# VectorE alone forms the token block sums, a down tile precedes the last block product, eight banks for the last chunk pair

## The reference, cut to what matters

```python
xn = rms_norm(x, g_pre_mix)
z  = xn @ w_in                       # 1024 tokens, 1024 -> 8192 columns
y_attn = diff_attention(q, k, v)     # 8 heads, two score maps each, per-head norm
y_conv = gb * short_conv(gc * hc)
y_pool = multiscale_pool(u)
gates  = sigmoid(z[..., OFF_GATE:] + b_gate)
merged = gates0 * (y_attn @ w_attn_proj) + gates1 * (y_conv @ w_conv_proj) + gates2 * (y_pool @ w_pool_proj)
x  = x + rms_norm(merged @ w_out, g_post_mix)
hn = rms_norm(x, g_pre_ffn)
gu = hn @ w_gate_up                  # 1024 -> 2 * 2816
ff = (silu(gu[..., :D_FF]) * gu[..., D_FF:]) @ w_down
x  = x + rms_norm(ff, g_post_ffn)
```

## Time and profile before

| what | us |
|---|---|
| median of three runs | 1870.77 (1868.34 to 1870.95) |
| the profiled execution, whole | 1869.41 |
| its span, first to last instruction | 1867.8 |
| PE busy | 1799.5 (96%) |
| VectorE busy | 1148.4 (61%) |
| ScalarE busy | 688.1 (37%) |
| GpSimd busy | 258.8 (14%) |

### The profile page before, as it was taken

The page is one execution under the profiler, slowest core; times in us unless marked ns, Lnnn a source line. Parts: engine busy times, 40 slices in busy tenths (PEclk is TensorE's granted clock), DMA queues, the critical chain, the costliest instruction groups (busy, mean ns, idle before and its releaser), DMA issues. The chain is left out here.

```text
span 1867.8 us, 25127 instructions
## 1 busy us (share of the span) xinstructions
PE 1799.5 (96%) x8628; PEld 1485.1 (80%) x8628; DVE 1148.4 (61%) x1778; ACT 688.1 (37%) x1351; POOL 258.8 (14%) x502
## 2 busy tenths in 40 slices
PE   6999999999989999999999999899999999999987
PEld 5877777777867888888888888688888888788876
DVE  4218888888765774441646645955545454567666
ACT  4216666666633323342221133433333333212111
POOL 2211111111150001112100112500000000000002
PEclk9999999999999999999999999999999999999999
DMA  6221111111132213337535513122222221333332
GB/s 218 91 57 35 58 58 56 57 56 45 57 124 79 90 62 107 113 102 281 187 120 183 204 68 113 56 74 82 81 68 95 79 95 68 124 124 112 124 113 90
DMA packets 123088, 187.11 MB, mean 100 GB/s; under 512 B 5936, under 2 KB 93488, under 8 KB 121984
## 3 DMA queue, kind: packets, MB, share of 16 engines
q1 hardware_dynamic: 99376, 99.36, 16.8%
q0 software_dynamic: 23344, 85.69, 12.5%
q10 hardware_dynamic: 288, 1.05, 0.2%
HBM read 136.79 MB, written 49.28 MB: 100 GB/s over the span
## 5 line engine op out<-in xcount | busy, mean ns | idle before, releaser
L2068 PE MATMUL ps<-w_d,hn 128*128 128x512 f32 x1008 | 228.8, 389 | 0.0
L2068 PEld LDWEIGHTS ps<-w_d,hn 128*128 128x128 f32 x1008 | 189.3, 188 | 39.3
L2134 PE MATMUL ps<-xn,ring 128*128 128x512 f32 x864 | 214.0, 398 | 1.4 <-DVE qt L1460 1.0
L2134 PEld LDWEIGHTS ps<-xn,ring 128*128 128x128 f32 x864 | 158.4, 189 | 32.8 <-issue 1.1
L2377 PE MATMUL ps<-s_op,t_op_T 128*128 128x512 f32 x720 | 169.9, 389 | 0.0
L2377 PEld LDWEIGHTS ps<-s_op,t_op_T 128*128 128x128 f32 x720 | 135.2, 188 | 28.1
L2243 PE MATMUL ps<-s_op,x_op_T 128*128 128x512 f32 x540 | 129.9, 395 | 9.5 <-DVE x_op_T L1387 9.5
L2243 PEld LDWEIGHTS ps<-s_op,x_op_T 128*128 128x128 f32 x540 | 102.9, 191 | 31.4 <-issue 9.9
L2009 DVE TENSOR_TENSOR ff_sum<-ff_sum,ps 128x512 f32<-128x512 f32 x128 | 87.9, 686 | 52.5 <-PE ps L2068 52.5
L2377 PE MATMUL ps<-hn,t_op_B 128*128 128x512 f32 x480 | 115.2, 389 | 0.0
L2377 PEld LDWEIGHTS ps<-hn,t_op_B 128*128 128x128 f32 x480 | 90.1, 188 | 18.7
(11 more groups left out here) (229 smaller groups left out, 3233.7 us busy)
## 6 DMA issues: line engine op xcount, KB each, us to landing
pair<-in_w_gate_up_dram SPq DMA_DIRECT2D x20, 1024.0 KB, 5.1
x_pair<-in_w_in_dram SPq DMA_DIRECT2D x15, 1024.0 KB, 6.3
raw<-in_w_in_dram SPq DMA_DIRECT2D x28, 512.0 KB, 4.1
raw_down<-in_w_down_dram SPq DMA_DIRECT2D x22, 512.0 KB, 3.5
raw_down<-hf_scratch SPq DMA_DIRECT2D x22, 512.0 KB, 3.2
hf_scratch<-hf_out POOLq DMA_DIRECT2D x40, 256.0 KB, 2.3
gate_in<-gate_scratch POOLq DMA_DIRECT2D x18, 512.0 KB, 3.6
y_scratch<-y_out POOLq DMA_DIRECT2D x8, 1024.0 KB, 4.2
```

The costliest lines, as they stand in the source:

```text
L2068: last = pe.matmul(ps[:, bank, :], lhs, rhs, start=i == 0, stop=i == len(pairs) - 1)
L2134: last = pe.matmul(ps[:, proj_bank(first, half), :], ring[:, which, a, P * k:P * (k + 1)], xn[:, b, k, HALF * half:HALF * (half + 1)], sta ...
```

## The change

VectorE forms all four token block sums, and all whole blocks, in both stages; POOL forms none. In the attention's end VectorE's instructions for them are set between the four last steps: two whole blocks before `step_of(0, 1, lag=2)`, one sum and one whole block before `step_of(0, 2, lag=3)`, one sum before `step_of(0, 3, lag=4)`. In the feed-forward one whole block comes before the last `hn_lo`, the rest after it. ACT takes the copies in another order, with fewer waits between them, and copies the first block sum ahead of a weight tile. In the last quad ACT and DVE split the operands of chunk 0 earlier, and PE runs the first down tile before the last B22 product. The last chunk pair holds eight groups in eight banks instead of four in four. ACT's square of the last norm writes its unused output to `row` and no longer to PSUM. The diff, cut to its core:

```diff
@@ gpsimd, attention's end
             pool.wait_ge(gates_first, 2)
-            pool.wait_ge(pv_done, HEADS * TT)
-            xn_whole(s_raw[2][:, HH], 0, 0)
             for m in range(2):
                 pool.dma_start(gate_dram[P * m:P * (m + 1), :], merged[:, m, :]).then_inc(early_stored[0], 16)
-            xn_whole(s_raw[1][:, HH], 1, 1)
-            xn_whole(s_raw[4][:, HH], 1, 0)
...
-            pool.wait_ge(xs_summed, 3)
-            pool.wait_ge(xs_added, 3)
-            pool.tensor_tensor(s_raw[4][:, LL], s_raw[4][:, HH], s_raw[2][:, LL], ALU.subtract).then_inc(xs_added, 1)
@@ gpsimd, feed-forward: the same four instructions and their waits removed
-            whole(s_raw[2][:, HH], 0, 0)
-            whole(s_raw[4][:, HH], 1, 0)
...
-            whole(s_raw[1][:, HH], 1, 1)
...
@@ scalar, attention's end
+            act.wait_ge(gates_first, 2)
+            act.wait_ge(xs_summed, 2)
+            x_s_hi(3)
             split_next()
-            act.wait_ge(xs_summed, 1)
-            x_s_hi(3)
+            act.wait_ge(xs_summed, 3)
+            x_s_hi(1)
+            x_s_hi(2)
             act.wait_ge(y_stored[0], 16 * HEADS // 2)
             sigmoid_half(part_of(stage, 0, 0), bias_g[:, 4:5])
...
-            act.wait_ge(xs_added, 4)
+            act.wait_ge(xs_summed, 4)
             x_s_hi(4)
@@ scalar, last ff_quad
                     t_hi_of("B11", 1 - kind)
+                else:
+                    for f in range(2):
+                        split_down(w_d[:, 0, HH, f, :])
+                    for f in range(2):
+                        split_down(hf_tile(0, HH, f))
                 act.wait_ge(products_done, pr.at(after(first, "P6")))
                 bank_copy(a2_copy, alpha)
...
@@ scalar, last norm
-                act.activation(junk, ff_sum[:, i, :], ACT.Square, accum_out=ssq[:, i % 2, 3:4])\
+                act.activation(row[:, :], ff_sum[:, i, :], ACT.Square, accum_out=ssq[:, i % 2, 3:4])\
@@ vector, attention's end
+            def whole(dst, a, kh, half):
+                s = slice(HALF * half, HALF * (half + 1))
+                did(dve.tensor_tensor(dst, a[:, HH, 4 * kh:4 * kh + 4, s].bitcast(F32),
+                                      a[:, LL, 4 * kh:4 * kh + 4, s].bitcast(F32), ALU.add))
...
             step_of(0, 0, lag=1)
+            whole(s_raw[2][:, LL], xn, 0, 0)
+            whole(s_raw[3][:, HH], xn, 0, 1)
             step_of(0, 1, lag=2)
             split_next()
+            x_s_sum(3, s_raw[2][:, LL], s_raw[3][:, HH], ALU.subtract)
+            whole(s_raw[1][:, HH], xn, 1, 1)
             step_of(0, 2, lag=3)
+            dve.wait_ge(pv_done, HEADS * TT)
+            x_s_sum(1, s_raw[3][:, HH], s_raw[1][:, HH], ALU.add)
             step_of(0, 3, lag=4)
...
+            dve.wait_ge(xs_summed, 2)
+            x_s_sum(2, s_raw[1][:, LL], s_raw[2][:, LL], ALU.subtract)
+            x_s_lo(3, 1)
             split_next()
...
             dve.wait_ge(x_pair_landed[0], 16)
             dve.wait_ge(y_stored[1], 16 * HEADS // 2)
...
+            dve.wait_ge(xs_summed, 3)
             x_s_lo(1, 2)
+            whole(s_raw[4][:, HH], xn, 1, 0)
+            x_s_sum(4, s_raw[4][:, HH], s_raw[2][:, LL], ALU.subtract)
             x_lo_of("T3", 0)
             x_lo_of("B11", 0)
@@ vector, feed-forward's start
             residual(1, TT - 1, last=True)
+            dve.wait_ge(groups_done, G_FFN)
+            whole(s_raw[2][:, LL], hn, 0, 0)
             hn_lo(TT - 1)
...
+            whole(s_raw[3][:, HH], hn, 0, 1)
+            s_sum(3, s_raw[2][:, LL], s_raw[3][:, HH], ALU.subtract)
+            whole(s_raw[1][:, HH], hn, 1, 1)
             hidden(0, 1)
             split_next()
+            s_sum(1, s_raw[3][:, HH], s_raw[1][:, HH], ALU.add)
             dve.wait_ge(s_summed, 2)
+            s_sum(2, s_raw[1][:, LL], s_raw[2][:, LL], ALU.subtract)
             g.next()
             hidden(1, 1)
...
             split_next()
+            s_lo_of(3, 1)
...
             t_sum("T1", 0)
+            whole(s_raw[4][:, HH], hn, 1, 0)
+            s_sum(4, s_raw[4][:, HH], s_raw[2][:, LL], ALU.subtract)
             t_lo_of("T3", 0)
             t_lo_of("B11", 0)
@@ vector, last ff_quad
+                if last:
+                    split_down(lambda s: w_d[:, 0, s, 0, :])
+                    split_down(lambda s: w_d[:, 0, s, 1, :])
                 dve.wait_ge(products_done, pr.at(after(first, "P2")))
                 combine(kind, 0, 0, gamma, a1_copy, 2, 1)
...
                 else:
+                    split_down(lambda s: hf_tile(0, s, 0))
+                    split_down(lambda s: hf_tile(0, s, 1))
                 dve.wait_ge(products_done, pr.at(after(first, "P4")))
                 combine(kind, 0, 1, beta, a2_copy, 3, 2)
@@ tensor
-            third(BANKS[1][0])
...
-            down((0,), 0)
+            pe.wait_ge(w_lo, n.at())
+            pe.wait_ge(combined, 3 * QUADS - 1)
+            down_tile((0,), 0)
+            third(BANKS[1][0])
+            for i in range(1, TT):
+                down_tile((0,), i)
...
-            for j in range(4):
-                wait_evacuated(pe, g, j - 4)
+            for j in range(8):
+                if j < 4:
+                    wait_evacuated(pe, g, j - 4)
                 for k in range(6):
-                    down_part(1, j // 2, j % 2, k, g.slot(4, j), start=k == 0)
+                    down_part(1, j // 2, j % 2, k, j, start=k == 0)
...
-            for j in range(4):
+            for j in range(8):
                 for k in range(6):
-                    last = down_part(0, j // 2, j % 2, k, g.slot(4), stop=k == 5)
+                    last = down_part(0, j // 2, j % 2, k, j, stop=k == 5)
...
-            down((1, 0), 0, first=2)
+            down((1, 0), 0, first=4)
```

More of the change, by code:

```diff
@@ L295, in build @@
         u_landed = sem("u_landed")
-        s_added, s_summed, s_hi, s_lo = sem("s_added"), sem("s_summed"), sem("s_hi"), sem("s_lo")
+        s_summed, s_hi, s_lo = sem("s_summed"), sem("s_hi"), sem("s_lo")
         pair_landed = [sem(f"pair_landed{b}") for b in range(2)]
@@ L762, in _ @@
             residual(1, TT - 1, last=True)
[L765 to L772, removed]
-            whole(s_raw[2][:, HH], 0, 0)
-            whole(s_raw[4][:, HH], 1, 0)
-            pool.wait_ge(tr_free[1], TT + HEADS * (TT + TT // 2) + TT)
-            whole(s_raw[1][:, HH], 1, 1)
-            pool.wait_ge(s_summed, 3)
-            pool.wait_ge(s_added, 2)
-            pool.tensor_tensor(s_raw[4][:, LL], s_raw[4][:, HH], s_raw[2][:, LL], ALU.subtract).then_inc(s_added, 1)
             for b in range(2):
@@ L1274, in ff_quad @@
                     t_hi_of("B21", 1 - kind)
-                else:
-                    for f in range(2):
-                        split_down(w_d[:, 0, HH, f, :])
                 if kind == 0:
@@ L1285, in ff_quad @@
                     t_hi_of("T4", 1 - kind, True)
-                else:
-                    for f in range(2):
-                        split_down(hf_tile(0, HH, f))
                 if kind == 0:
@@ L1314, in _ @@
             g.next()
-            act.wait_ge(s_summed, 1)
-            s_hi_of(3)
             silu_half(1)
@@ L1320, in _ @@
             act.wait_ge(s_summed, 2)
+            s_hi_of(3)
             s_hi_of(1)
@@ L1333, in _ @@
                 silu_half(half)
+                if half == 0:
+                    act.wait_ge(s_summed, 4)
+                    s_hi_of(4)
             t_hi_of("B21", 0)
@@ L1689, in _ @@
             x_lo_of("T4", 0)
+            x_s_lo(4, 4)
             g.next(4)
@@ L1917, in ff_quad @@
                     t_lo_of("T4", 1 - kind)
-                else:
-                    split_down(lambda s: hf_tile(0, s, 0))
                 dve.wait_ge(products_done, pr.at(after(first, "P5")))
                 combine(kind, 1, 1, alpha, b1_copy, 1, 3)
-                if last:
-                    split_down(lambda s: hf_tile(0, s, 1))
                 if kind == 1:
@@ L1941, in s_lo_of, with s_sum @@
                 lo(s_op[kept][:, LL], s_raw[kept][:, LL], s_op[kept][:, HH]).then_inc(s_lo, 1)
+            def s_sum(kept, in0, in1, op):
+                dve.tensor_tensor(s_raw[kept][:, LL], in0, in1, op).then_inc(s_summed, 1)
             g.next()
[L1944 removed]
             dve.wait_ge(tr_free[0], TT + HEADS * TT + TT)
[L1946 to L1952 removed]
+            dve.wait_ge(tr_free[1], TT + HEADS * (TT + TT // 2) + TT)
+            whole(s_raw[3][:, HH], hn, 0, 1)
+            s_sum(3, s_raw[2][:, LL], s_raw[3][:, HH], ALU.subtract)
+            whole(s_raw[1][:, HH], hn, 1, 1)
             hidden(0, 1)
             split_next()
+            s_sum(1, s_raw[3][:, HH], s_raw[1][:, HH], ALU.add)
             dve.wait_ge(s_summed, 2)
[L1956 to L1957 removed]
+            s_sum(2, s_raw[1][:, LL], s_raw[2][:, LL], ALU.subtract)
             g.next()
@@ L1969, in _ @@
             t_sum("T1", 0)
-            s_lo_of(1, 2)
-            dve.wait_ge(s_added, 4)
-            s_lo_of(2, 3)
```

(18 more changed lines are left out.)

40 lines of the change are left out of this document (4 added, 36 removed).

## The result

| | before | after |
|---|---|---|
| median of 4 runs, us | 1869.6 (1868.3 to 1871.0) | 1843.5 (1842.7 to 1845.0) |
| profiled execution, span | 1867.8 | 1841.1 |

The ratio is 0.9861, 95% interval 0.9846 to 0.9877: the change makes the kernel 1.4% faster, 26 us. The forecast was 1839 with a range of 1834 to 1848.

A forecast was written before the change was run, and what follows sets the result against it. PE's list of instructions was taken as the time, with losses where PE waits and then runs at slow clock. Gains 9.5 + 8.5 + 5.1 + 7.7 = 30.8 us gave 1838.6 or 1840.0, said as 1839; range 1834 to 1848.

The forecast's parts named there:

- the four places: PE's losses at attention's end, feed-forward's start, last B22 product and last chunk pair: gains 9.5, 8.5, 5.1 and 7.7 us.
- part 1: Attention's end: 12.0 us lost before quad 0 and to slow clock; all but a new 2.5 goes, gain 9.5.
- part 2: Feed-forward's start: waits for the last row and a weight tile, and slow clock, go: 3.4 + 3.3 + 1.8 = 8.5 us.
- The slower rival: Long block sums are VectorE's own, not POOL's doing; kernel slower from 5.0 us per block instruction, 1880 at 5.56; chance 0.03.
- why it is late: Attention's end: the sum at L1668 takes 11.39 us instead of 2.28, since DVE stood until POOL's block sums were through.
- the new stall of 2.5: Attention's end: PE's transposition waits 2.5 us for a bank freed by tile 6's `y_lo`, behind a sum and whole block.
- The clock behind that stall: Attention's end: slow clock after PE's new 2.5 us wait, bounds 0 and 2.4 us, taken as 0.
- Part 3: Last B22 product: 6.4 us lost before, a stall of 1.3 left before the first down tile; gain 5.1 (3 to 6.2).
- Part 4: Last chunk pair: 48 matmuls fill the wait for chunk 10's operands; of 7.8 us lost, 0.1 wait left; gain 7.7.
- The head's store: Attention's end: store issued 3.5 us later lands in 10.2, weight pairs in 11.3; T3 at 550.9, hidden with 3.8 to spare.
- the rival of the late store: Attention's end: store sharing DMA with gates takes 20.4 us, lands at 550.8, T3 6.0 late, total 1847.4; chance 0.08.
- The first rival: Clock falls behind the new 2.5 us stall (2.4) and hidden tiles land two us late (2.0): 1843.4; forecast's width together 0.80.

The follow-up runs named there:

- The two undone parts: Changed kernel with the last pair put back to four groups in four banks, 1851.3 us; with the last quad's splits and product order put back, 1846.4 us.

## Why the prediction held, and where it missed

**What bounds it, and the four places**: right. The two undone parts cost 8 and 3 us, POOL's single block 4. The prediction's walks of VectorE's list came out too: for the feed-forward's start they have a weight tile ready at 1187.9 and 1196.2 and T3 at 1206; taken 6.7 us earlier, as after's trace stands here, that is 1181.2, 1189.5 and 1199.3, and it was 1181.4, 1189.6 and 1199.6.

**POOL's block sums as the cause of part 1's and part 2's waits**: right. For part 2 the run with one block back on POOL shows it. For part 1 no run puts POOL's sums back; there it rests on the two traces, in which every block instruction takes 2.28 to 2.29 once POOL forms none. The slower rival needed 5.0. The prediction's "why it is late" names L1668 alone; the weight sum of 4.89 us held T3 back by another 4.2.

**Part 1, the new stall of 2.5**: its cause is right and shown by the two runs that move the sums; its wait was 2.50. From start to start it is 2.7 (526.1 to 528.85), since the modelled end of the half job lies 0.25 after the point at which the next instruction could start. T3 was ready at 551.9, forecast 550.9 with the whole timeline 1.4 later here.

**The clock behind that stall, "I take 0"**: a term that was mis-sized. The forecast looked for one answer, and there are two. The same wait of 2.5 us is in eight traces: behind it PE lost 0 in four of them and 1.3, 1.3, 1.6 and 1.6 in the others, 0.7 on the mean. The bound of 2.4 was never reached.

**Part 2**: 8.5 forecast, 8.5 measured.

**Part 3, 5.1, measured 3.9**: the step that failed is "The copy that this sum needs stands behind the hidden tiles on ACT's list, at 1598.8, in time." The time is right: after's trace is 15.2 us earlier here, so the forecast is 1583.6, and it ended at 1583.3. "In time" is not. Not only the sum needs this copy, the last T1 product does as well, since it writes the same bank, and PE wanted to start it at 1580.95. PE's list holds the wait for it (`copied`) just ahead of that product, and I followed the operands, not this. So the stall is 2.4 us and one product earlier, not 1.3 before the down tile. The run with the copy moved shows it, and also the rest of the old reckoning: with the copy out of the way PE waits 0.85 before the down tile, forecast 1.3. Behind the 2.2 to 2.7 us waits of this kind in seven traces PE lost 0.1 in three, with the clock up, and 1.7, 1.7, 1.7 and 3.0 in four, 1.2 on the mean. The forecast had none, because this wait was not in it. Its "the clock stayed up after shorter waits" held for the waits of up to 1.0 us, not for this one.

**Part 4**: 7.7 forecast, 7.5 measured. That VectorE would give part of it back at the end, the rival of the run with four banks, didn't happen: after PE's last matmul the tail has 12.4 us in both kernels.

**The head's store**: it landed 10.3 us after its issue, forecast 10.2, with both weight pairs (12.7 as the median, forecast 11.3) and three of the four gate stores issued within 2.2 us of it. It doesn't bind in the changed kernel, and it is the nearest limit once the stall is gone. In the rival of the late store the landing at 550.8 is 0.6 later than 529.8 + 20.4; nothing hangs on it.

**The sum**: 1839 became 1843.5. Of the 4.5 us, 1.1 are the T1 wait above the forecast stall, 1.9 the clock behind the two waits on the mean, 0.4 the small differences in the new stall and in part 4. The last 1.1 isn't settled; the kernel's start alone varies by more. The first rival's 1843.4 is met by luck: it wants the clock to take 2.4 behind the new stall and the hidden tiles to land two us late. The clock took 0.7 there on the mean, and ScalarE began on the hidden tiles at 1579.61 and 1581.75, where the forecast landings, 15.2 earlier, are 1579.7 and 1581.9.

## What to carry to other kernels

When an instruction is moved on one engine, list everything that waits for what stands behind it, and look through the consumer's own waits: a copy out of a PSUM bank has two consumers, the sum that uses the copy and the next product that overwrites the bank. Long instructions go behind the short one that another engine waits for: two of 2.28 us ahead of a step of 0.6 us made a stall of 2.5, and the same two behind it cost nothing. Adds of SBUF blocks given half to VectorE and half to GpSimd weren't shared here: one of VectorE with two of POOL took until 11.4 us after its start, and three on VectorE alone take 6.8 (1172.05 to 1178.87 in after).

## What the runs showed of the hardware

Behind one and the same PE wait of 2.2 to 2.7 us the granted clock either stays or falls to about half for 1.3 to 3 us of lost time, and differs between executions of one kernel: 8 of 15 such waits, in ten traces, were followed by a slow stretch. Waits up to 1.0 us never were. Two waits of 3.3 us went both ways too: nothing lost in the kernel before, 2.8 us in the run with a block on POOL. So a wait of 2.2 to 2.7 us costs about one microsecond more than it shows (1.0, the mean of the 15), and removing it can gain more than its length: 4.3 us for the one of 2.2. What decides between the two outcomes no run here shows.

GpSimd held back VectorE's instruction with two SBUF inputs when it read SBUF itself, and not when it only wrote: an add of 4.53 us held a 1.28 us instruction until its end, a memset of 1.80 us over the same stretch didn't touch it. The other way round the traces show it too. In the changed kernel two of POOL's small instructions at the attention's end take 1.83 and 2.60 us while VectorE forms two whole blocks (512.97 to 517.58), instead of 0.19 and 0.55:

```profile
513.47 1.83 POOL L605 TENSOR_SCALAR o_scale<-o_ssq 128x1 f32<-128x1 f32 x1 [7.52 <-ACT junk_o L922]
515.38 2.60 POOL L606 TENSOR_TENSOR o_scale<-o_scale,minus_half 128x1 f32<-128x1 f32 x1
```
